# One product of 512 columns over high and low halves of the tokens in the gate of the second feed-forward network

## The chip, the cores and the metric

The kernel runs on one core of a Trainium2 chip. The metric is the device time of one execution in microseconds (us), the median of several runs. All matrix products are done on TensorE (PE); ScalarE (ACT) evaluates functions and copies, VectorE (DVE) does the element-wise arithmetic, SyncE (SP) issues the transfers of the weights and GpSimd (POOL) those of one further weight matrix.

## The reference

Two layers (`DEPTH = 2`) of a transformer block over 256 tokens with 1024 features. In each layer two gated feed-forward networks stand around a token mixing. Everything is float32. The part that the change touches is the gate `g` of the second network:

```python
def swiglu(h, w_gate, w_up, w_down):
    g = jnp.einsum('bsd,df->bsf', h, w_gate)
    u = jnp.einsum('bsd,df->bsf', h, w_up)
    return jnp.einsum('bsf,fd->bsd', jax.nn.silu(g) * u, w_down)

for l in range(DEPTH):
    h = modulate(rms_norm(x, norm_ffn1[l]), sh1, sc1)
    x = x + 0.5 * g1 * swiglu(h, w_gate1[l], w_up1[l], w_down1[l])
    h = modulate(rms_norm(x, norm_mix[l]), sh2, sc2)
    x = x + g2 * token_mixing(h, ...)
    h = modulate(rms_norm(x, norm_ffn2[l]), sh3, sc3)
    x = x + 0.5 * g3 * swiglu(h, w_gate2[l], w_up2[l], w_down2[l])
```

`D_FF` is 2816. The shifts, scales and gates (`sh1` to `g3`) are a product of `silu(c)` with `w_ada`, a matrix of 1024 x 9216 for each layer.

## The kernel before

**High and low parts.** A float32 product is made of three products in a reduced format (fp32r): each operand is split into a high part (rounded by ACT: `whi`, `hhi`, `guhi`) and a low part (the rest, by DVE: `wlo`, `hlo`, `gulo`), and `three` (L1282) adds high x high, high x low and low x high into one bank of PSUM. The stationary operand is the weight for the gate and the up product, the moving one is `hhi` or `hlo`, 128 features by 256 tokens, so each of these products has 256 columns.

**Steps.** Each feed-forward network is cut into 11 steps (`NF`) of 256 of its 2816 columns. `which` is 0 for the first network and 1 for the second. In a step i of the network (numbered from 0) PE does, in this order, the gate (48 products of 256 columns into bank `GB`), the up product (48 of 256 columns into `UB0` and `UB1`) and the down product (24 of 512 columns into four banks). Their weights come in three slots: slot 0 the gate's, slot 1 the up's, slot 2 the down's. Step 0 has another order of its own (`as_they_come`, banks `GB` and `SB_`), the last step puts two products between up and down (`spread_gate`), and steps 1 to 9 are a loop.

**ACT and DVE in a step.** Both engines do their work in the order in which it is written. In a step i > 0 of the second network ACT waits for the gate's end (`g_done`), evaluates silu over 512 columns of `GB` (L516), then rounds the down weights of this step (`split_hi(2)`, L464, a copy of 128 x 2048), then waits for DVE's product and rounds its first half to `guhi` (L520), rounds the gate weights of the next step (slot 0), and does the same for the second half and for slot 1. DVE weighs a chunk of `w_ada` first (`weigh_ada`, L801 and L803, 8 operations), then waits for `split_hi(2)` and makes the first half of `wlo[2]` (L997), waits for silu and for the first half of the up product, multiplies (L1002), waits for `guhi` and makes `gulo` (L1004), makes the second half of `wlo[2]` (L1006), then the same for the second half, and at last the low parts of slots 0 and 1 for the next step (L873). PE waits for the first `gulo` (`gulo_ready`, L1462) ahead of the down product, and for the low weights of slot 0 and 1 (`split_done`) ahead of gate and up.

**Late chunks.** In steps 0 and 1 of the second network DVE weighs a further chunk of `w_ada` (`weigh_late`, L850) between the low parts of slot 0 and slot 1. In layer 0 every step i > 0 begins with `weigh_ada`; in layer 1 steps 1 and 2 alone do.

Of the kernel before, what the change touches and what calls it, by code (L numbers as in the profile page):

```python
# [8 lines left out]
F32R = mybir.dt.float32r  # L9
BF16 = mybir.dt.bfloat16  # L10
I32 = mybir.dt.int32
ALU = mybir.AluOpType
ACT = mybir.ActivationFunctionType
AX_X = mybir.AxisListType.X

P = 128
# [19 lines left out]
def build(nc, x, c, w_ada, b_ada, norm_ffn1, w_gate1, w_up1, w_down1, norm_mix, w_in, qn_a, kn_a, qn_c, kn_c,  # L36
          g_out, w_out, norm_ffn2, w_gate2, w_up2, w_down2, out):
    _, S, D = x.shape
    L = w_in.shape[0]
    FF = w_gate1.shape[2]  # L40
    KT = D // P
    TT = S // P
    NF = FF // CW
# [42 lines left out]
    with ctx:  # L86
        def sb(name, shape, dt=F32):
            return ctx.enter_context(nc.sbuf_tensor(name, shape, dt))

        def sem(name):  # L90
            return ctx.enter_context(nc.semaphore(name))
# [6 lines left out]
        xs = sb("xs", [P, TT, D])  # L98
        xn = sb("xn", [P, TT, D])
        hTf = sb("hTf", [P, KT, S])  # L100
        hhi = sb("hhi", [P, KT, S], F32R)
        hlo = sb("hlo", [P, KT, S], F32R)
        gate = sb("gate", [P, D])
        room = sb("room", [P, 24, S])
        sqr = sb("sqr", [P, 2, S])
# [16 lines left out]
        eb = sb("eb", [P, GRP * (S + P)])  # L122
# [40 lines left out]
        mid_early = xn[:, 0, 0:2 * CW].rearrange("p (a n) -> p a n", a=2)  # L163
        silu = eb[:, 0:2 * S]
        guf = eb[:, 2 * S:4 * S]
        zf = hTf[:, :, :].rearrange("p k s -> p (k s)")
        z0 = zf[:, 0:GRP * S].rearrange("p (h s) -> p h s", h=GRP)
        z1 = zf[:, GRP * S:GRP * (S + P)].rearrange("p (h s) -> p h s", h=GRP)
# [9 lines left out]
        GB, UB0, UB1, SB_ = PS[4], PS[5], PS[6], PS[7]  # L178
# [55 lines left out]
        out_done = sem("out_done")  # L234

        g_done = sem("g_done")
        silu_ready = sem("silu_ready")
        u_done = sem("u_done")
        gu_ready = sem("gu_ready")
# [69 lines left out]
        def turn(l, n):  # L309

            return l * U_LAYER + n
# [141 lines left out]
        def _(act):  # L453
# [54 lines left out]
            def ffn_step(l, which, i, ahead, after, gated=False):  # L508
                base = turn(l, U_FFN[which])
                n = i + nth(l, 2 * NF, which * NF)  # L510
                act.wait_ge(g_done, n + 1)
                if gated:
                    act.activation(silu[:, 0:S], GB[:, 0:S], ACT.Silu)
                    act.activation(silu[:, S:2 * S], SB_[:, 0:S], ACT.Silu).then_inc(silu_ready, 1)
                else:
                    act.activation(silu, GB[:, :], ACT.Silu).then_inc(silu_ready, 1)  # L516
                split_hi(2, i + base)
                for ft in range(2):
                    act.wait_ge(gu_ready, n * 2 + ft + 1)
                    act.activation(guhi[:, ft * S:(ft + 1) * S], guf[:, ft * S:(ft + 1) * S], ACT.Copy).then_inc(guhi_ready, 1)  # L520
                    if after is not None:
                        split_hi(ft, i + after if ahead else after)
# [154 lines left out]
            for l in range(L):  # L677
# [49 lines left out]
                for n in range(NSLOT, len(OUT_CHUNKS)):  # L727
# [3 lines left out]
                    k = n % NSLOT  # L731
# [11 lines left out]
        def _(dve):  # L743
# [243 lines left out]
            def ffn_step(l, which, i, ahead, after, weighs=True, first=False, late=None):  # L987
                base = turn(l, U_FFN[which])
                n = i + nth(l, 2 * NF, which * NF)
                if which == 0 and not first:  # L990
                    weigh_ada([i + ada_turn(l, k, 0) for k in range(2)], [0, 1],
                              held[:, at_cols(i * (2 * CW) - 2 * CW, 2 * CW)].rearrange("p (a n) -> p a n", a=2))
                elif which == 1 and weighs and not first:
                    weigh_ada([i + ada_turn(l, 0, WF1 + 2)], [0], held[:, at_cols(i * CW + CW, CW)].rearrange("p (a n) -> p a n", a=1))

                dve.wait_ge(hi_full[2], i + (base + 1))
                dve.tensor_tensor(wlo[2][:, 0:D], raw[2][:, 0:D], whi[2][:, 0:D].bitcast(F32), ALU.subtract)  # L997
                dve.wait_ge(silu_ready, n + 1)
                for ft in range(2):
                    cut = slice(ft * S, (ft + 1) * S)  # L1000
                    dve.wait_ge(u_done, n * 2 + ft + 1)
                    dve.tensor_tensor(guf[:, cut], silu[:, cut], (UB0, UB1)[ft][:, 0:S], ALU.mult).then_inc(gu_ready, 1)  # L1002
                    dve.wait_ge(guhi_ready, n * 2 + ft + 1)
                    dve.tensor_tensor(gulo[:, cut], guf[:, cut], guhi[:, cut].bitcast(F32), ALU.subtract).then_inc(gulo_ready, 1)  # L1004
                    if ft == 0:
                        dve.tensor_tensor(wlo[2][:, D:2 * D], raw[2][:, D:2 * D], whi[2][:, D:2 * D].bitcast(F32), ALU.subtract).then_inc(split_done[2], 1)  # L1006
                if ahead:
                    split_lo(0, i + after)
                    if late is not None:
                        weigh_late(l, late)  # L1010
                    split_lo(1, i + after)
# [162 lines left out]
            for l in range(L):  # L1174
# [81 lines left out]
                for n in range(NSLOT, len(OUT_CHUNKS)):  # L1256
# [3 lines left out]
                    k = n % NSLOT  # L1260
# [11 lines left out]
        def _(pe):  # L1272
            pe.wait_ge(tables, 1)
            pe.wait_ge(rows_in, 5 * 16)
            for l in range(L):
                for k in range(KT):

                    o = (l * KT + k) * 13
                    last = pe.transpose(PS[0][:, o:o + 13], rows[:, l, k * P:(k + 1) * P], ident[0:13, 0:13])
            last.then_inc(cols_done, 1)  # L1280

            def three(ps, l_hi, l_lo, r_hi, r_lo, first, last):  # L1282

                pe.matmul(ps, l_hi, r_hi, start=first, stop=False)  # L1284
                pe.matmul(ps, l_hi, r_lo, start=False, stop=False)  # L1285
                return pe.matmul(ps, l_lo, r_hi, start=False, stop=last)  # L1286
# [137 lines left out]
            def ffn_step(l, which, i, is_last, first=False):  # L1424
                use = i + turn(l, U_FFN[which])
                n = i + nth(l, 2 * NF, which * NF)
                if first and (l > 0 or which > 0):
                    as_they_come(l, 2 * which, use, (GB, SB_)).then_inc(g_done, 1)
                elif not first:
                    pe.wait_ge(split_done[0], use + 2)  # L1430
                    wh, wl = chunk_cols(whi[0]), chunk_cols(wlo[0])
                    for ft in range(2):
                        for k in range(KT):
                            last = three(GB[:, ft * S:(ft + 1) * S], wh[:, k, ft * P:(ft + 1) * P], wl[:, k, ft * P:(ft + 1) * P],
                                         hhi[:, k, :], hlo[:, k, :], k == 0, k == KT - 1)
                    last.then_inc(g_done, 1)
                if first:
                    low_weights_last(use, UB0[:, 0:S]).then_inc(u_done, 1)
                else:
                    pe.wait_ge(split_done[1], use + 2)  # L1440
                wh, wl = chunk_cols(whi[1]), chunk_cols(wlo[1])
                for ft in range(1 if first else 0, 2):
                    for k in range(KT):
                        last = three((UB0, UB1)[ft][:, 0:S], wh[:, k, ft * P:(ft + 1) * P], wl[:, k, ft * P:(ft + 1) * P],
                                     hhi[:, k, :], hlo[:, k, :], k == 0, k == KT - 1)
                    last.then_inc(u_done, 1)
                if is_last:

                    pe.wait_ge(silu_ready, n + 1)
                    spread_gate(l, 2 * which, 0)  # L1450

                def down(ft, t, close):
                    tok = slice(ft * S + t * P, ft * S + (t + 1) * P)
                    for half in range(2):
                        w = slice(ft * D + half * HALF, ft * D + (half + 1) * HALF)
                        last = three(DB[2 * t + half][:, :], guhi[:, tok], gulo[:, tok], whi[2][:, w], wlo[2][:, w], first and ft == 0, close)
                        if close:
                            last.then_inc(d_done, 1)
                    return last


                pe.wait_ge(gulo_ready, n * 2 + 1)  # L1462
                if is_last:

                    spread_gate(l, 2 * which, 1)
                    down(0, 0, False)
                else:
                    for t in range(TT):
                        down(0, t, False)
                pe.wait_ge(split_done[2], use + 2)  # L1470
                pe.wait_ge(gulo_ready, n * 2 + 2)
                if is_last:
                    down(1, 0, True)
                    down(0, 1, False)
                    down(1, 1, True)
                else:
                    for t in range(TT):
                        down(1, t, False)
# [183 lines left out]
            for p in range(4):  # L1662
                last = gate_pair(p)
            last.then_inc(g_done, 1)
            pe.sem_inc(modc_done, 1)
            for l in range(L):
# [6 lines left out]
                for n in range(NC):  # L1673
# [5 lines left out]
                    if n == 3:  # L1679
# [3 lines left out]
                        for t in range(TT):  # L1683
                            last = pe.transpose(PVB[:, 8 + t * H_I:8 + (t + 1) * H_I], wiT[:, t * P:(t + 1) * P], ident[HD:KW, HD:KW])
# [39 lines left out]
                for n, (k0, nk) in enumerate(OUT_CHUNKS[:-1]):  # L1724
                    slot = n % NSLOT
                    pe.wait_ge(split_done[slot], turn(l, U_OUT + n // NSLOT) + 2)
                    if n == 0:

                        for low in (False, True):
                            for t in range(TT):  # L1730
                                pe.wait_ge(y_lo if low else y_hi, nth(l, 4, t + 1))
                                tok = slice(t * P, (t + 1) * P)
                                for half in range(2):
                                    w = slice(half * HALF, (half + 1) * HALF)
                                    if low:
                                        last = pe.matmul(DB[2 * t + half][:, :], hlo[:, k0, tok], whi[slot][:, w], start=False, stop=False)  # L1736
# [7 lines left out]
                    if n < 4:  # L1744
                        for t in range(TT):
                            last = out_block(n, t)
                        last.then_inc(out_done, 1)
                pe.wait_ge(y_lo, nth(l, 4, 4))
                for t in range(TT):
                    last = out_block(4, t)  # L1750
# [33 lines left out]
```

## Time and profile before

| | |
|---|---|
| Median of 3 runs | 1160.73 us (1159.63 to 1160.75) |
| Profiled execution | 1162.37 us |
| its span, first to last instruction | 1160.6 us |
| PE busy | 1132.1 us, 98% |
| DVE busy | 867.7 us, 75% |
| ACT busy | 530.2 us, 46% |
| TensorE clock, mean of the span | 0.992 of full |
| Products of 256 columns of `three` with the weight stationary | 3 x 1600 |

The busy shares are sums over the span; what an engine is worth in a stage is read from the timeline of the stage. The second network of layer 0 lies at about 404 to 593 us, that of layer 1 at about 966 to 1155 us. A duration of a matrix product in the timeline includes its way through the array; products overlap, so the rate is read from the distance of two starts.

### The profile page before, as it was taken

What the parts mean: (1) busy time and instruction counts of PE and PEld (TensorE: products, weight loads), DVE (VectorE), ACT (ScalarE), POOL (GpSimd) and SP (SyncE); (2) the same over time, 40 slices, a digit from 0 to 9 for tenths busy, and PEclk for the clock granted to TensorE, in tenths of its full rate; (3) what the DMA queues carried; (4) which work ended last, traced back from release to release, by engine and by line L of the source; (5) the groups of instructions that cost most, each with busy time, mean ns of one, the idle gap of its engine ahead of it and who ended that gap; (6) DMA issues with size and microseconds to landing.
All of it is one profiled execution on the core that took longest, in us unless ns stands there. A gap on an engine that the chain in (4) does not pass through costs nothing.

```text
span 1160.6 us, 20192 instructions
## 1 busy us (share of the span) xinstructions
PE 1132.1 (98%) x7890; PEld 1022.0 (88%) x7890; DVE 867.7 (75%) x1281; ACT 530.2 (46%) x685; POOL 64.5 (6%) x79
## 2 busy tenths in 40 slices
PE   6999999999999999999999999999999999999998
PEld 3699999989988799999989999997998878899997
DVE  5688788788986787766777787777888777845545
ACT  3433433555655653343364334435456555433432
POOL 2000110100000000000000101100000000000000
PEclk9999999999999999999989999998999999999999
DMA  9889889946532577777837898893943253756451
GB/s 304 282 287 319 293 296 331 314 128 214 182 99 91 174 234 252 251 236 257 270 129 256 294 333 297 296 348 114 299 146 128 92 181 113 235 196 211 154 196 73
DMA packets 160373, 258.43 MB, mean 223 GB/s; under 512 B 8365, under 2 KB 127277, under 8 KB 160319
## 3 DMA queue, kind: packets, MB, share of 16 engines
q1 hardware_dynamic: 140739, 182.25, 47.4%
q0 software_dynamic: 19584, 75.50, 19.4%
q8 instruction: 32, 0.52, 0.2%
q14 instruction: 18, 0.15, 0.0%
HBM read 256.56 MB, written 1.05 MB: 222 GB/s over the span
## 4 chain that ended last, share of the span: by engine, by line
PE 75%; DVE 12%; DMA 4%; ACT 3%; DVEq 3%; issue 2%; SPq 0%; ACTq 0%; POOLq 0%; POOL 0%
PE bank L1284 21%; PE bank L1286 20%; PE bank L1285 20%; DVE wlo L873 4%; DVE room L803 3%; DMA ada<-in_w_ada_dram 2%; PE bank L1628 2%; DVEq L805 1%; DMA raw<-in_w_gate_dram 1%; ACT whi L464 1%; PE bank L1547 1%; PE bank L1339 1%; PE bank L1375 1%; DMA xs<-in_x_dram 1%; PE bank L1404 1%
## 5 line engine op out<-in xcount | busy, mean ns | idle before, releaser
L1284 PE MATMUL bank<-hhi,whi 128*128 128x256 f32 (+1 forms) x1600 | 454.9, 284 | 0.0
L1286 PE MATMUL bank<-hhi,wlo 128*128 128x256 f32 (+1 forms) x1600 | 452.4, 283 | 0.0
L1285 PE MATMUL bank<-hlo,whi 128*128 128x256 f32 (+1 forms) x1600 | 452.2, 283 | 0.0
L464 ACT ACTIVATE whi<-raw 128x2048 fp32r<-128x2048 f32 (+1 forms) x174 | 321.7, 1851 | 9.8 <-PE bank L1736 5.3
L1284 PEld LDWEIGHTS bank<-hhi,whi 128*128 128x128 f32 (+1 forms) x1600 | 305.8, 191 | 4.0 <-issue 1.8
L1285 PEld LDWEIGHTS bank<-hlo,whi 128*128 128x128 f32 (+1 forms) x1600 | 305.9, 191 | 2.4 <-issue 0.5
L1286 PEld LDWEIGHTS bank<-hhi,wlo 128*128 128x128 f32 (+1 forms) x1600 | 305.8, 191 | 0.0
L873 DVE TENSOR_TENSOR wlo<-raw,whi 128x2048 fp32r<-128x2048 f32 (+2 forms) x130 | 281.9, 2197 | 12.1 <-ACT whi L464 10.7
L516 ACT ACTIVATE eb<-bank 128x512 f32<-128x512 f32 x40 | 23.9, 598 | 336.9 <-PE bank L1286 336.9
L803 DVE SCALAR_TENSOR_TENSOR room<-ada,cT,room 128x512 f32 (+3 forms) x252 | 159.5, 633 | 19.1
L997 DVE TENSOR_TENSOR wlo<-raw,whi 128x1024 fp32r<-128x1024 f32 x44 | 53.9, 1225 | 129.2 <-ACT whi L464 128.1
L1284 PE MATMUL bank<-whi,guhi 128*128 128x512 f32 x352 | 141.5, 402 | 1.7 <-DVE gulo L1004 1.7
L1285 PE MATMUL bank<-wlo,guhi 128*128 128x512 f32 x352 | 139.2, 395 | 0.0
L1286 PE MATMUL bank<-whi,gulo 128*128 128x512 f32 x352 | 139.2, 395 | 0.0
L422 POOL DMA_DIRECT2D ada<-in_w_ada_dram x64 | 56.3, 883 | 909.9 <-DVEq L837 758.9
L1284 PEld LDWEIGHTS bank<-whi,guhi 128*128 128x128 f32 x352 | 66.3, 188 | 17.8 <-DVE gulo L1004 2.5
L1286 PEld LDWEIGHTS bank<-whi,gulo 128*128 128x128 f32 x352 | 66.2, 188 | 16.1
L1285 PEld LDWEIGHTS bank<-wlo,guhi 128*128 128x128 f32 x352 | 66.2, 188 | 14.8 <-issue 1.0
L520 ACT ACTIVATE guhi<-eb 128x256 fp32r<-128x256 f32 x88 | 36.8, 418 | 87.3 <-DVE eb L1002 86.6
L1004 DVE TENSOR_TENSOR gulo<-eb,guhi 128x256 fp32r<-128x256 f32 x88 | 37.5, 426 | 42.6 <-ACT guhi L520 42.6
L1284 PE MATMUL bank<-whi,hhi 128*128 128x256 f32 (+1 forms) x184 | 60.5, 329 | 0.8 <-DVE wlo L873 0.8
L1285 PE MATMUL bank<-wlo,hhi 128*128 128x256 f32 (+1 forms) x184 | 58.0, 315 | 0.0
(224 smaller groups left out, 1164.5 us busy)
## 6 DMA issues: line engine op xcount, KB each, us to landing
ada<-in_w_ada_dram POOLq DMA_DIRECT2D x68, 1024.0 KB, 5.9
raw<-in_w_gate_dram SPq DMA_DIRECT2D x44, 1024.0 KB, 5.6
raw<-in_w_up_dram SPq DMA_DIRECT2D x44, 1024.0 KB, 7.0
raw<-in_w_down_dram SPq DMA_DIRECT2D x44, 1024.0 KB, 5.1
raw<-in_w_in_dram SPq DMA_DIRECT2D x28, 1024.0 KB, 6.4
raw<-in_w_out_dram SPq DMA_DIRECT2D x8, 512.0 KB, 3.3
raw<-in_w_out_dram SPq DMA_DIRECT2D x4, 1024.0 KB, 7.0
room<-in_w_ada_dram POOLq DMA_DIRECT2D x3, 1024.0 KB, 14.1
```

Source lines behind the costliest of these rows:

```text
L422: pool.dma_start(ada[:, slot, :, :], v_ada[:, row, col]).then_inc(ada_full[slot], 16)
L464: last = act.activation(dst, src, ACT.Copy)
L516: act.activation(silu, GB[:, :], ACT.Silu).then_inc(silu_ready, 1)
L520: act.activation(guhi[:, ft * S:(ft + 1) * S], guf[:, ft * S:(ft + 1) * S], ACT.Copy).then_inc(guhi_ready, 1)
L803: last = dve.scalar_tensor_tensor(sums, chunks[:, :, k, :], cT[:, k:k + 1], sums, ALU.mult, ALU.add)
L873: last = dve.tensor_tensor(dst, src, hi.bitcast(F32), ALU.subtract)
L997: dve.tensor_tensor(wlo[2][:, 0:D], raw[2][:, 0:D], whi[2][:, 0:D].bitcast(F32), ALU.subtract)
L1004: dve.tensor_tensor(gulo[:, cut], guf[:, cut], guhi[:, cut].bitcast(F32), ALU.subtract).then_inc(gulo_ready, 1)
L1284: pe.matmul(ps, l_hi, r_hi, start=first, stop=False)
L1285: pe.matmul(ps, l_hi, r_lo, start=False, stop=False)
L1286: return pe.matmul(ps, l_lo, r_hi, start=False, stop=last)
L1628: last = pe.matmul(PV_BANK[n][:, h * HD:(h + 1) * HD], probs(b, h), vs[:, b, off + h * HD:off + (h + 1) * HD], start=(b == 0), stop=(b == t))
```

## The change

In the second network (`which == 1`), steps 1 to 10 of both layers, the gate is computed in another way; step 0, the up and down products and the whole first network stay. `hhi` and `hlo` become two halves of one tile, side by side for each group of 128 features, so that they can be read as 512 moving columns. For each high weight one product of 512 columns then gives high x high in the first 256 columns of a bank and high x low in the other 256; low weight x high tokens, 256 columns, is added to the first 256. The two groups of 128 gate columns go to two banks, `GB` and `SB_`. The gate is then the sum of the two halves of each bank: ACT copies the second halves to a tile `gsum` in SBUF, DVE adds the first halves to it, and ACT evaluates silu over `gsum`.

```diff
-        hhi = sb("hhi", [P, KT, S], F32R)
-        hlo = sb("hlo", [P, KT, S], F32R)
+        both_h = sb("both_h", [P, KT, 2, S], F32R)
+        hhi, hlo = both_h[:, :, 0, :], both_h[:, :, 1, :]
...
+        gsum = eb[:, 4 * S:6 * S]
...
# ACT, ffn_step
+                elif which == 1:
+                    for ft in range(2):
+                        act.activation(gsum[:, ft * S:(ft + 1) * S], (GB, SB_)[ft][:, S:2 * S], ACT.Copy).then_inc(glow_read, 1)
+                    act.wait_ge(gsum_ready, i + l * (NF - 1))
+                    act.activation(silu, gsum, ACT.Silu).then_inc(silu_ready, 1)
                 else:
                     act.activation(silu, GB[:, :], ACT.Silu).then_inc(silu_ready, 1)
                 split_hi(2, i + base)
...
# DVE, ffn_step, behind weigh_ada
+                if which == 1 and not first:
+                    for ft in range(2):
+                        g = gsum[:, ft * S:(ft + 1) * S]
+                        dve.wait_ge(glow_read, i * 2 + (l * 2 * (NF - 1) + ft - 1))
+                        last = dve.tensor_tensor(g, (GB, SB_)[ft][:, 0:S], g, ALU.add)
+                    last.then_inc(gsum_ready, 1)
                 dve.wait_ge(hi_full[2], i + (base + 1))
                 dve.tensor_tensor(wlo[2][:, 0:D], raw[2][:, 0:D], whi[2][:, 0:D].bitcast(F32), ALU.subtract)
...
# PE, ffn_step, the gate
+                        cut = slice(ft * P, (ft + 1) * P)
                         for k in range(KT):
+                            if which == 1:
+                                bank = (GB, SB_)[ft]
+                                pe.matmul(bank[:, :], wh[:, k, cut], both_h[:, k, :, :].rearrange("p a s -> p (a s)"), start=k == 0, stop=False)
+                                last = pe.matmul(bank[:, 0:S], wl[:, k, cut], hhi[:, k, :], start=False, stop=k == KT - 1)
+                                continue
                             last = three(GB[:, ft * S:(ft + 1) * S], wh[:, k, ft * P:(ft + 1) * P], wl[:, k, ft * P:(ft + 1) * P],
                                          hhi[:, k, :], hlo[:, k, :], k == 0, k == KT - 1)
```

On PE, at the head of the loop over the second network's steps, the gate before, for one group of features:

```order
L1483 ISA
L1284 MATMUL bank<-hhi,whi 128x256
L1285 MATMUL bank<-hlo,whi 128x256
L1286 MATMUL bank<-hhi,wlo 128x256
L1284 MATMUL bank<-hhi,whi 128x256
```

and now, where both halves are named `both_h`:

```order
L1503 ISA
L1451 MATMUL bank<-both_h,whi 128x512
L1452 MATMUL bank<-both_h,wlo 128x256
L1451 MATMUL bank<-both_h,whi 128x512
L1452 MATMUL bank<-both_h,wlo 128x256
```

Sixteen pairs stand where sixteen triples stood; the columns streamed are the same.

On ACT, at the head of the same loop, before (`eb` holds silu, its product and now `gsum`; `bank` is PSUM):

```order
L527 UNCONDITIONAL_BRANCH
L527 ISA
L516 ACTIVATE eb<-bank 128x512
L460 ISA
L464 ACTIVATE whi<-raw 128x2048
L519 ISA
L520 ACTIVATE guhi<-eb 128x256
```

and now:

```order
L535 UNCONDITIONAL_BRANCH
L535 ISA
L520 ACTIVATE eb<-bank 128x256 x2
L522 ACTIVATE eb<-eb 128x512
L463 ISA
L467 ACTIVATE whi<-raw 128x2048
L527 ISA
L528 ACTIVATE guhi<-eb 128x256
```

Two copies stand ahead of silu, and silu and all behind it, the rounding of the down weights (L467) first, come behind a wait for DVE.

On DVE, in the same loop of layer 0, before:

```order
L801 TENSOR_SCALAR room<-ada,cT 128x256
L803 SCALAR_TENSOR_TENSOR room<-ada,cT,room 128x256 x7
L996 REGISTER_ALU
L997 TENSOR_TENSOR wlo<-raw,whi 128x1024
L1001 ISA
L1002 TENSOR_TENSOR eb<-eb,bank 128x256
```

and now:

```order
L809 TENSOR_SCALAR room<-ada,cT 128x256
L811 SCALAR_TENSOR_TENSOR room<-ada,cT,room 128x256 x7
L1007 ISA
L1008 TENSOR_TENSOR eb<-bank,eb 128x256 x2
L1010 REGISTER_ALU
L1011 TENSOR_TENSOR wlo<-raw,whi 128x1024
```

The two additions stand behind the eight operations of `weigh_ada` and ahead of the first half of `wlo[2]`.

## Rows read from the trace of the kernel before

**Rows 1.** The page: busy times, and the chain that ended last.

```profile
PE 1132.1 (98%) x7890; PEld 1022.0 (88%) x7890; DVE 867.7 (75%) x1281; ACT 530.2 (46%) x685; POOL 64.5 (6%) x79
PE 75%; DVE 12%; DMA 4%; ACT 3%; DVEq 3%; issue 2%; SPq 0%; ACTq 0%; POOLq 0%; POOL 0%
```

**Rows 2.** Timeline of PE, step 6, layer 0: start, duration (us), engine, line, operation.

```profile
506.17 0.28 PE L1284 MATMUL bank<-hhi,whi 128*128 128x256 f32 x1
...
511.91 0.28 PE L1284 MATMUL bank<-hhi,whi 128*128 128x256 f32 x1
...
517.55 0.28 PE L1286 MATMUL bank<-hhi,wlo 128*128 128x256 f32 x1
517.66 0.40 PE L1284 MATMUL bank<-whi,guhi 128*128 128x512 f32 x1
...
523.27 0.28 PE L1284 MATMUL bank<-hhi,whi 128*128 128x256 f32 x1
```

**Rows 3.** Timeline of ACT, the same step; in brackets its idle time and releaser.

```profile
512.11 0.60 ACT L516 ACTIVATE eb<-bank 128x512 f32<-128x512 f32 x1 [8.48 <-PE bank L1286]
512.60 1.90 ACT L464 ACTIVATE whi<-raw 128x2048 fp32r<-128x2048 f32 x1
516.12 0.42 ACT L520 ACTIVATE guhi<-eb 128x256 fp32r<-128x256 f32 x1 [1.62 <-DVE eb L1002]
```

**Rows 4.** Timeline of DVE, the same step.

```profile
514.53 1.23 DVE L997 TENSOR_TENSOR wlo<-raw,whi 128x1024 fp32r<-128x1024 f32 x1 [3.67 <-ACT whi L464]
515.68 0.41 DVE L1002 TENSOR_TENSOR eb<-eb,bank 128x256 f32<-128x256 f32 x1
516.58 0.43 DVE L1004 TENSOR_TENSOR gulo<-eb,guhi 128x256 fp32r<-128x256 f32 x1 [0.48 <-ACT guhi L520]
516.92 1.22 DVE L1006 TENSOR_TENSOR wlo<-raw,whi 128x1024 fp32r<-128x1024 f32 x1
```

**Rows 5.** Timeline of ACT, step 0; last, a group by line (count, busy, mean ns).

```profile
408.10 0.39 ACT L513 ACTIVATE eb<-bank 128x256 f32<-128x256 f32 x1 [0.67 <-PE bank L1409]
408.38 0.38 ACT L514 ACTIVATE eb<-bank 128x256 f32<-128x256 f32 x1
...
L627 ACT ACTIVATE hhi<-hTf 128x512 fp32r<-128x512 f32 x8 | 4.7, 624 | 5.6 <-DVE hTf L913 5.6
```

**Rows 6.** Timelines of DVE and PEld (weight loads), steps 0 to 3, layer 0.

```profile
410.59 1.23 DVE L997 TENSOR_TENSOR wlo<-raw,whi 128x1024 fp32r<-128x1024 f32 x1 [1.54 <-ACT whi L464]
...
428.58 1.23 DVE L997 TENSOR_TENSOR wlo<-raw,whi 128x1024 fp32r<-128x1024 f32 x1
...
442.57 3.84 DVE L803 SCALAR_TENSOR_TENSOR room<-ada,cT,room 128x256 f32 x7
446.63 1.23 DVE L997 TENSOR_TENSOR wlo<-raw,whi 128x1024 fp32r<-128x1024 f32 x1 [0.22 <-issue]
...
449.15 0.19 PEld L1284 LDWEIGHTS bank<-whi,guhi 128*128 128x128 f32 x1 [0.89 <-DVE gulo L1004]
...
463.24 1.23 DVE L997 TENSOR_TENSOR wlo<-raw,whi 128x1024 fp32r<-128x1024 f32 x1 [3.18 <-ACT whi L464]
```

**Rows 7.** Timeline of ACT: silu of steps 1, 2, 3 and 10, layer 0.

```profile
425.20 0.60 ACT L516 ACTIVATE eb<-bank 128x512 f32<-128x512 f32 x1 [8.41 <-PE bank L1286]
...
442.75 0.60 ACT L516 ACTIVATE eb<-bank 128x512 f32<-128x512 f32 x1 [7.97 <-PE bank L1286]
...
460.81 0.60 ACT L516 ACTIVATE eb<-bank 128x512 f32<-128x512 f32 x1 [7.99 <-PE bank L1286]
...
580.51 0.60 ACT L516 ACTIVATE eb<-bank 128x512 f32<-128x512 f32 x1 [8.48 <-PE bank L1286]
```

**Rows 8.** Timelines, last step of layer 0: PE between up and down; DVE behind.

```profile
586.07 1.88 PE L1347 MATMUL bank<-room,ones 128*128 128x512 f32 x4
...
588.05 1.29 DVE L865 TENSOR_TENSOR gate<-bank,LG 128x512 f32<-128x512 f32 x2 [0.27 <-PE bank L1347]
```

**Rows 9.** Windows: length; busy PE, PEld, DVE, ACT, POOL; clock; DMA share, GB/s.

```profile
237.00:242.00 5.00, 5.00 (x26) 3.86 (x26) 2.56 (x10) 1.45 (x5) 0.00 (x0) 0.66 0.00 0
1155.46:1159.40 3.94, 0.00 (x0) 0.00 (x0) 1.94 (x3) 0.00 (x0) 0.00 (x0) 1.00 0.60 243
1159.40:1160.60 1.20, 0.00 (x0) 0.00 (x0) 0.00 (x0) 0.00 (x0) 0.00 (x0) 0.54 0.19 75
```

## Prediction made before the change was run

> **What bounds the kernel now.** The page comes first: PE is busy for 98% of the span and holds 75% of the chain that ended last [rows 1]. A busy PE says little by itself, so the timeline of an ordinary step of the second network comes next: step 6 of layer 0. Gate, up and down follow each other without a gap: the gate's first product starts at 506.17, the up's at 511.91, the down's at 517.66, the next gate's at 523.27 [rows 2]. The step is 17.10 us long and all of it is PE's. The distance of two starts is (517.66 - 511.91) / 48 = 0.1198 us for 256 columns, and for 512 columns (523.27 - 517.66) / 24 = 0.234 us (the down product is 24 of them) [rows 2]. So time is taken by columns, and two products of 256 columns cost only 0.006 us more than one of 512.
>
> The third view is what PE would wait for if it were late: the first `gulo` ahead of the down product. Its chain in this step: silu at 512.11, rounding of the down weights at 512.60 [rows 3], first half of `wlo[2]` at 514.53 (DVE had stood idle for 3.67 us for it), product at 515.68, `gulo` at 516.58 for 0.43 us [rows 4], so it is there at 517.01. PE starts loading the first weights of the down product as the last up product starts, at 517.55 [rows 2]. The slack is about 0.5 us.
>
> The fourth view is the same chain in a step in which it is late. In step 2, DVE is still weighing `w_ada` (from 442.57 for 3.84 us), `wlo[2]` starts at 446.63 and PE's weight load for the down product stands idle for 0.89 us until 449.15, 2.52 us behind the start of `wlo[2]` [rows 6]. The step before and this one are 17.55 and 18.06 us long by silu's starts [rows 7], 0.45 and 0.96 us over 17.10. From this I take a rule of cost: let x be the start of L997; the down product behaves as if it started at x + 2.62, or where the up product ends, if that is later. In step 2 the up product ends at 442.75 - 0.20 + 5.75 = 448.30, and 446.63 + 2.62 - 448.30 = 0.95, which is the row's 0.96.
>
> **Part 1, the gate's products.** Removed are 48 starts of 256 columns, 5.74 us [rows 2]; added are 16 of 512 and 16 of 256. The mixture does not occur. With 0.234 and 0.1198 it takes 5.66 us; if PE's 256-column products cost half a 512 (0.117) once fewer instructions are queued, 5.61; bounds for the gain are 0 and 0.2 us. I take 5.61, a gain of 0.13 us in each of 20 steps, 2.6 us in all. The Trainium skill (TensorE: Matmul & The Clock Gate, Back-to-back issue gap) gives a warm product N/2.4 ns plus a fixed 2.5 ns; the rows differ from it (0.234 us where it has 0.216), and by it the gain would be 16 x 2.5 ns = 0.04 us for each step.
>
> **Part 2, the way to silu in an ordinary step.** Let A be the time at which ACT sees the gate's end. Before, silu starts at A, the rounding at A + 0.49, L997 at A + 2.42 [rows 3, 4]. Now: the first copy takes 0.39 us, the second starts 0.28 behind it [rows 5]; a handoff takes 0.03 us (512.60 + 1.90 to 514.53 [rows 3, 4]); the first addition starts at A + 0.42, the second 0.34 later (516.58 to 516.92 is that distance [rows 4]), and takes 0.41 us like the 256-column product with a PSUM operand [rows 4]: done at A + 1.17. Silu starts at A + 1.20. From SBUF 512 columns take 0.62 us [rows 5], and as now the next operation starts 0.11 before the end: rounding at A + 1.71, L997 at A + 3.64. That is 1.22 us later. DVE would otherwise be idle in that time (the 3.67 us above), so no work of its own is pushed. But queued behind ACT's new wait is the rounding of the down weights, and behind that, on DVE, the whole chain to `gulo`. PE has 517.66 - (514.53 + 2.62) = 0.51 us of slack [rows 2, 4] and then waits 0.71 us. With the gain of part 1 the step is 0.58 us longer: 17.68 us. From x to the next x by parts: 2.62 (start of down) + 5.61 + 5.61 + 0.20 + 3.64 = 17.68. The second `gulo` follows x by 4.9 us, PE wants it 2.7 us behind the start of the down product, at x + 5.3, so it costs nothing more; the low parts for the next gate are done at x + 7.1, wanted at x + 8.2. Bounds for the delay: 0.85 (the two copies and additions overlap better) to 1.6 us (a handoff of 0.15 us each).
>
> **Part 3, steps 1 and 2 with late chunks.** There DVE is the one that is late: L997 starts as soon as the weighing is done. The additions now stand in front of it, ACT's wait for them ends later still, and the rounding of the down weights, until now long done, begins only then: from the end of the weighing 0.34 + 0.41 + 0.03 + 0.51 + 1.93 = 3.22 us to L997, where it was 0. In step 1 x moves from 428.58 to 431.80; in step 2 by another 3.22, as the weighing there ends at a fixed distance behind the x of step 1 (446.63 - 428.58 = 18.05, all DVE's [rows 6]). PE then waits 3.8 us in step 1 and 4.3 us in step 2. Step 3 starts from PE again: x to x was 463.24 - 446.63 = 16.61 [rows 6] and becomes 17.68, 1.07 more. Bounds: 3.0 to 3.5 us for each of the two.
>
> **Part 4, the last step.** Between up and down PE has products of `spread_gate` (4 records, 1.88 us [rows 8]), the first half ahead of its wait for `gulo`. They cover the 1.22 us of delay within 0.2 us, so it drops out of the sum. DVE's end of the chain moves the gate's addition (588.05 [rows 8]) by 1.2, of which 0.3 us reach the residual; at the end of layer 0 PE's own work covers that, at the end of layer 1 it counts.
>
> **Sum for a layer.** 3.22 + 3.22 + 1.07 + 7 x 0.58 (x of steps 4 to 10) = 11.57; less 1.22 for the last step = 10.35 us. Layer 1 has the same two late chunks and the same distances; that its later steps don't weigh changes nothing, as DVE is ahead there. Both: 20.7, and 0.3 at the end: 21.0 us. The sum is made against the span of 1160.6 us; the profiled execution's own time, 1162.37, is 1.77 above its span and 1.6 above the median. A step's length is the same in all runs, so the difference goes onto the median: 1160.73 + 21.0 = 1181.7, say **1182 us**.
>
> **Rivals.** (a) The clock falls in the pauses. At the kernel's end PE rests from 1155.46; the granted clock is 1.00 until 1159.40 and mostly at half (1.2 GHz) in the 1.2 us behind [rows 9]: the trace shows a fall some 4 us into a rest. The pause of step 2 is 4.3 us, that of step 1 3.8. Where it fell elsewhere it stayed low for (1 - 0.66) x 5 x 2 = 3.4 us [rows 9]; a fall in step 2 costs half of that, 1.7 us (in step 1 DVE's chain covers it). One layer: 1183.7; both: 1185.4. The Trainium skill (TensorE: Matmul & The Clock Gate, HAM oscillation) describes just this, pauses between groups of products after which each group starts at half clock; by it both layers pay, 1185.4. (b) The delay is hidden, since PE's slack is larger than I read: then only part 1 is left, 2.6 us, and the time is 1158.1, faster. It decides at a slack of 1.22 us; the 0.89 us that PE did wait in step 2 speaks against. (c) Only the ordinary steps pay, because DVE reaches its additions earlier in steps 1 and 2 than I count: 20.7 less 2 x (3.22 + 3.22 - 1.16) = 10.1, 1171. (d) The product of 512 columns is no faster and the handoffs are slow: 1.6 us of delay, no gain: 2 x (3.5 + 3.5 + 1.6 + 7 x 1.1 - 1.6) = 29, 1190. (e) The change does nothing, the gate being built as before: 1160.7; the order of instructions shows it is not so.
>
> **How the numbers follow.** Forecast 0.60, (a) 0.22, (b) 0.03, (c) 0.07, (d) 0.06, (e) 0.02. The low bounds (0.85 us of delay, 3.0 for the late steps) give 2 x (3.0 + 3.0 + 0.7 + 7 x 0.2 - 0.85) = 14.5, 1175; the high ones (1.6 us, 3.5) give 2 x (3.5 + 3.5 + 1.5 + 7 x 0.96 - 1.6) = 27, 1188, and (a) lies within. The range is 1175 to 1188. Differences under 0.2% (2.3 us) can't be told from none: faster 0.03, same 0.02, slower 0.95.
>
> **What would show it.** In the changed profile PE's weight load ahead of the down product should stand idle in 18 steps with DVE's `gulo` as releaser, about 0.6 to 0.7 us in 14 of them and about 4 us in steps 1 and 2 of each layer; silu's starts should be 17.68 us apart; the gate's 32 products should take 5.6 us; ACT should stand in a wait for DVE ahead of silu. Step lengths of 17.0 in the second network would refute parts 2 and 3, an idle of 0.9 us in step 2 part 3 alone, a granted clock at half behind step 2 would be (a).

## The result and the profile after

The changed kernel took 1184.37 us in the median of 4 runs (1181.62 to 1187.43), the kernel before 1160.18 us (4 runs): 24.2 us more, a ratio of 1.021 (95% interval 1.0194 to 1.0227). The forecast was 1182, between 1175 and 1188.

The page of the changed kernel, against [rows 1]. PE has 6.5 us more of busy time in a span that is 23.0 us longer, and ACT holds 7% of the chain that ended last, where it held 3%:

```profile
span 1183.6 us, 19663 instructions
PE 1138.6 (96%) x7570; PEld 1010.7 (85%) x7570; DVE 883.4 (75%) x1321; ACT 544.5 (46%) x725; POOL 64.7 (5%) x79
PE 71%; DVE 12%; ACT 7%; issue 4%; DVEq 2%; DMA 2%; SPq 0%; ACTq 0%
```

The waits (total us, times, longest): the row that answers the question what PE waits for, first of the kernel before, then of the changed kernel. Before, this wait came 4 times and made 2.5 us; now it comes in all 18 steps of the two loops:

```profile
PEld bank L1284 <- DVE gulo L1004: 2.5, 4, 0.9
...
PEld bank L1298 <- DVE gulo L1018: 21.9, 18, 4.2
```

**An ordinary step** (step 7 of layer 0), timelines of ACT, DVE, PE's weight loads (PEld) and PE, against [rows 2 to 4]:

```profile
538.06 0.66 ACT L520 ACTIVATE eb<-bank 128x256 f32<-128x256 f32 x2 [7.78 <-PE bank L1452]
539.27 0.63 ACT L522 ACTIVATE eb<-eb 128x512 f32<-128x512 f32 x1 [0.55 <-DVE eb L1008]
539.80 1.90 ACT L467 ACTIVATE whi<-raw 128x2048 fp32r<-128x2048 f32 x1
...
538.48 0.76 DVE L1008 TENSOR_TENSOR eb<-bank,eb 128x256 f32<-128x256 f32 x2 [0.96 <-ACT eb L520]
541.74 1.22 DVE L1011 TENSOR_TENSOR wlo<-raw,whi 128x1024 fp32r<-128x1024 f32 x1 [2.50 <-ACT whi L467]
543.78 0.43 DVE L1018 TENSOR_TENSOR gulo<-eb,guhi 128x256 fp32r<-128x256 f32 x1 [0.48 <-ACT guhi L528]
...
544.25 0.19 PEld L1298 LDWEIGHTS bank<-whi,guhi 128*128 128x128 f32 x1 [0.69 <-DVE gulo L1018]
...
549.96 0.39 PE L1451 MATMUL bank<-both_h,whi 128*128 128x512 f32 x1
...
555.61 0.28 PE L1298 MATMUL bank<-both_h,whi 128*128 128x256 f32 x1
```

From ACT's first copy (538.06) to silu are 1.21 us, to the rounding of the down weights 1.74, to the first half of `wlo[2]` 3.68; before, the last was 2.42. DVE stands idle for 2.50 us for ACT's rounding, and ACT for 0.55 us for DVE's additions ahead of it. The first weight load of the down product stands idle for 0.69 us. The gate is 555.61 - 549.96 = 5.65 us long, where it was 5.74.

**Steps 1 and 2** of layer 0, against [rows 6, 7]: rows of DVE and of PE's weight loads (PEld) in turn, and at the end ACT's copies at the gate's end of steps 1, 2, 3 and 10:

```profile
431.90 1.23 DVE L1011 TENSOR_TENSOR wlo<-raw,whi 128x1024 fp32r<-128x1024 f32 x1 [2.50 <-ACT whi L467]
...
434.41 0.29 PEld L1298 LDWEIGHTS bank<-whi,guhi 128*128 128x128 f32 x1 [3.84 <-DVE gulo L1018]
...
449.94 0.76 DVE L1008 TENSOR_TENSOR eb<-bank,eb 128x256 f32<-128x256 f32 x2 [0.22 <-issue]
453.20 1.23 DVE L1011 TENSOR_TENSOR wlo<-raw,whi 128x1024 fp32r<-128x1024 f32 x1 [2.50 <-ACT whi L467]
...
455.71 0.19 PEld L1298 LDWEIGHTS bank<-whi,guhi 128*128 128x128 f32 x1 [2.79 <-DVE gulo L1018]
...
425.07 0.66 ACT L520 ACTIVATE eb<-bank 128x256 f32<-128x256 f32 x2 [8.22 <-PE bank L1452]
447.41 0.66 ACT L520 ACTIVATE eb<-bank 128x256 f32<-128x256 f32 x2 [9.33 <-PE bank L1452]
467.26 0.66 ACT L520 ACTIVATE eb<-bank 128x256 f32<-128x256 f32 x2 [7.87 <-PE bank L1452]
...
591.21 0.66 ACT L520 ACTIVATE eb<-bank 128x256 f32<-128x256 f32 x2 [7.88 <-PE bank L1452]
```

From the additions (449.94) to `wlo[2]` (453.20) are 3.26 us, in which DVE itself works for 0.76. The steps are 22.34 and 19.85 us long, where they were 17.55 and 18.06. Steps 3 to 10 are (591.21 - 467.26) / 7 = 17.71 us long, where they were 17.10.

### The profile page after: what moved, and what is told of

The parts are those of the page before. It is cut to its first block, busy times and chain, and to the rows that moved or that the text cites. A ratio compares the mean times of both kernels' runs of the same rounds, so it can differ in the third digit from the quotient of the medians.

```text
span 1183.6 us, 19663 instructions
## 1 busy us (share of the span) xinstructions
PE 1138.6 (96%) x7570; PEld 1010.7 (85%) x7570; DVE 883.4 (75%) x1321; ACT 544.5 (46%) x725; POOL 64.7 (5%) x79
## 4 chain that ended last, share of the span: by engine, by line
PE 71%; DVE 12%; ACT 7%; issue 4%; DVEq 2%; DMA 2%; SPq 0%; ACTq 0%
PE bank L1298 17%; PE bank L1299 16%; PE bank L1300 16%; PE bank L1451 5%; ACT whi L467 4%; DVE wlo L881 3%; PE bank L1452 3%; DVE room L811 2%; PE bank L1648 2%; DVEq L813 1%; PE bank L1567 1%; DVE eb L1008 1%; PE bank L1353 1%; DMA xs<-in_x_dram 1%; DVE gulo L1018 1%
## 5 line engine op out<-in xcount | busy, mean ns | idle before, releaser
L1298 PE MATMUL bank<-both_h,whi 128*128 128x256 f32 (+1 forms) x1280 | 365.1, 285 | 0.0
L1299 PE MATMUL bank<-both_h,whi 128*128 128x256 f32 (+1 forms) x1280 | 362.6, 283 | 0.0
L1300 PE MATMUL bank<-both_h,wlo 128*128 128x256 f32 (+1 forms) x1280 | 362.6, 283 | 0.0
L467 ACT ACTIVATE whi<-raw 128x2048 fp32r<-128x2048 f32 (+1 forms) x174 | 321.7, 1850 | 8.0 <-PE bank L1756 5.3
L1298 PEld LDWEIGHTS bank<-both_h,whi 128*128 128x128 f32 (+1 forms) x1280 | 245.2, 192 | 4.0 <-issue 1.8
L1299 PEld LDWEIGHTS bank<-both_h,whi 128*128 128x128 f32 (+1 forms) x1280 | 245.2, 192 | 1.4 <-issue 0.5
L1300 PEld LDWEIGHTS bank<-both_h,wlo 128*128 128x128 f32 (+1 forms) x1280 | 245.3, 192 | 0.0
L1298 PE MATMUL bank<-whi,guhi 128*128 128x512 f32 x352 | 144.9, 412 | 18.3 <-DVE gulo L1018 18.3
L1451 PE MATMUL bank<-both_h,whi 128*128 128x512 f32 x320 | 113.1, 396 | 0.0
L524 ACT ACTIVATE eb<-bank 128x512 f32<-128x512 f32 x20 | 12.0, 598 | 169.3 <-PE bank L1300 169.3
L1452 PE MATMUL bank<-both_h,wlo 128*128 128x256 f32 x320 | 89.8, 280 | 0.0
L520 ACT ACTIVATE eb<-bank 128x256 f32<-128x256 f32 x40 | 13.2, 381 | 161.8 <-PE bank L1452 161.8
```

The source lines that it names most:

```text
L467: last = act.activation(dst, src, ACT.Copy)
L1451: pe.matmul(bank[:, :], wh[:, k, cut], both_h[:, k, :, :].rearrange("p a s -> p (a s)"), start=k == 0, stop=False)
L1452: last = pe.matmul(bank[:, 0:S], wl[:, k, cut], hhi[:, k, :], start=False, stop=k == KT - 1)
```

## The experiments

The theory: the loss isn't the work added but where ACT's wait for DVE stands. The rounding of the down weights is queued behind it, on that waits DVE's `wlo[2]`, and on that the `gulo` which PE wants first. PE has 0.5 us of slack there in an ordinary step; in steps 1 and 2 DVE is late already, and there is none. The rivals: the wide product or the shared tile costs; it is the load on DVE; it is the clock.

**The changed kernel again,** beside the three that follow.

> The changed kernel again, beside the others of this group. Theory (the wait of ScalarE for VectorE holds back the rounding of the down weights, and with it the first low product that TensorE wants): 1184 us, ordinary steps of the second network 17.70 us, 0.6 to 0.7 us of TensorE's idle time in each and about 4 us in steps 1 and 2. Rival (the half clock seen behind step 1 in both layers makes the loss): the time goes with the mean granted clock from run to run, and a run without a fall would be near 1180.

It took 1184.33 us (1183.53 to 1185.97, 4 runs); the kernel before, over 19 runs in the same group, 1159.45 us; ratio 1.0228 (1.0211 to 1.0245). Ordinary steps were (592.82 - 468.96) / 7 = 17.69 us. The clock is not what makes the loss, but it takes part. Windows of this run (length; PE, PEld, DVE, ACT, POOL; clock; DMA share, GB/s), the last two rows behind the pauses of step 2 in layer 0 and in layer 1:

```profile
433.40:440.00 6.60, 5.34 (x13) 4.19 (x14) 5.56 (x8) 4.44 (x4) 0.00 (x0) 0.50 0.52 179
...
457.00:461.00 4.00, 4.00 (x12) 3.13 (x11) 3.52 (x5) 2.48 (x3) 0.00 (x0) 0.57 0.58 213
...
1027.00:1031.00 4.00, 4.00 (x12) 3.12 (x11) 3.52 (x4) 3.08 (x3) 0.00 (x0) 0.57 0.48 161
```

From the gate's end of step 1 to that of step 3 this run needs 43.65 us in layer 0 (425.31 to 468.96), the first profiled run of the changed kernel 42.19. The first profiled run had the clock down in step 1 alone (in layer 0 from 434 to 438 us, mean 0.57), this one in step 2 too. So a fall in step 1 was covered and one in step 2 cost 1.5 us, as rival (a) had it.

**The sum without the wide product.**

```diff
 # the kernel before, which == 1, steps 1 to 10; on PE the two groups of gate columns go to two banks
+    for ft in range(2):
+        act.activation(gsum[:, ft * S:(ft + 1) * S], (GB, SB_)[ft][:, 0:S], ACT.Copy).then_inc(glow_read, 1)
+    act.wait_ge(gsum_ready, i + l * (NF - 1))
+    act.activation(silu, gsum, ACT.Silu, scale=0.5).then_inc(silu_ready, 1)
 ...
+    last = dve.tensor_tensor(g, (GB, SB_)[ft][:, 0:S], g, ALU.add)
```

> The three products of 256 columns as before, but the way to silu as in the changed kernel: ScalarE copies the gate's 512 columns in two pieces, VectorE adds the bank to the copy, silu takes half of the sum. Theory: all of the loss is here, and the gain of the wide product is missing in the 16 steps in which TensorE's length counts, 16 x 0.09 = 1.5 us: 1186 us, ordinary steps 17.8 us. Rival (the wide product or the shared tile is what costs): near 1160.

1186.65 us (1185.65 to 1189.04, 4 runs), ratio 1.0249 (1.023 to 1.0268). Steps 3 to 10 are 17.84 us long (470.25 to 595.15 for seven). So the loss is there without the wide product and without the shared tile: all of it is on the way to silu.

**The wide product without the sum.** This kernel leaves the second halves of the banks, high x low, out of the gate.

```diff
 # the changed kernel, which == 1, steps 1 to 10
-    two copies, wait for gsum_ready, silu of gsum; on VectorE the two additions
+    act.activation(silu[:, 0:S], GB[:, 0:S], ACT.Silu)
+    act.activation(silu[:, S:2 * S], SB_[:, 0:S], ACT.Silu).then_inc(silu_ready, 1)
```

> The wide products alone: the second halves of the banks are left out of the sum, silu reads the first halves straight from the two banks, no copy, no addition, no wait for VectorE. Theory: the gate takes 5.66 us instead of 5.75, so 20 x 0.09 = 1.8 us less than before: 1158.4 us, ordinary steps 17.01 us. Rival (the wide product costs): above 1161. Rival (a wide product saves much more than the rows show): below 1155.

1157.93 us (1155.04 to 1159.35, 10 runs), ratio 0.9984 (0.9968 to 1.0). The wide product doesn't cost; it saves more in a step than was expected (0.20 us instead of 0.09). PE's timeline in an ordinary step, first and last pair of the gate and the first up product:

```profile
504.76 0.39 PE L1443 MATMUL bank<-both_h,whi 128*128 128x512 f32 x1
504.99 0.28 PE L1444 MATMUL bank<-both_h,wlo 128*128 128x256 f32 x1
505.10 0.40 PE L1443 MATMUL bank<-both_h,whi 128*128 128x512 f32 x1
...
510.31 0.28 PE L1290 MATMUL bank<-both_h,whi 128*128 128x256 f32 x1
```

The gate is 510.31 - 504.76 = 5.55 us long, 0.347 for a pair, and a step 16.90 us (493.61 to 510.51 at silu), 0.20 less than before. In the changed kernel, where PE waits in each step, the same pairs take 5.65 us.

**The rounding ahead of the wait.**

```diff
 # ACT, the changed kernel, which == 1, steps 1 to 10
     two copies
+    split_hi(2, i + base)
     act.wait_ge(gsum_ready, i + l * (NF - 1))
     act.activation(silu, gsum, ACT.Silu).then_inc(silu_ready, 1)
-    split_hi(2, i + base)
```

> The changed kernel with one move: ScalarE rounds the down weights right behind its two copies, ahead of the wait for VectorE and of silu. Theory: the first half of the low down weights starts 2.5 us behind the gate's end as seen by ScalarE instead of 3.6, silu is ready ahead of its use, TensorE doesn't wait in ordinary steps (17.0 us); in steps 1 and 2 the additions alone remain, 0.75 us each: 1160.2 - 1.8 + 4 x 0.75 = 1161.4 us. Rival (the load of 40 additions on VectorE makes the loss, not the order on ScalarE): above 1175.

1158.97 us (1157.07 to 1161.45, 10 runs), ratio 0.9998 (0.9985 to 1.0011). With the same instructions in another order the whole loss is gone. ACT and DVE in an ordinary step of this kernel:

```profile
513.63 0.66 ACT L520 ACTIVATE eb<-bank 128x256 f32<-128x256 f32 x2 [8.21 <-PE bank L1454]
514.17 1.92 ACT L467 ACTIVATE whi<-raw 128x2048 fp32r<-128x2048 f32 x1
515.98 0.63 ACT L523 ACTIVATE eb<-eb 128x512 f32<-128x512 f32 x1
...
514.04 0.76 DVE L1010 TENSOR_TENSOR eb<-bank,eb 128x256 f32<-128x256 f32 x2 [1.40 <-ACT eb L520]
516.12 1.23 DVE L1013 TENSOR_TENSOR wlo<-raw,whi 128x1024 fp32r<-128x1024 f32 x1 [1.32 <-ACT whi L467]
```

`wlo[2]` starts 2.49 us behind the gate's end instead of 3.68, the additions run while ACT rounds, and silu runs while DVE makes `wlo[2]`. The steps are 16.90 us long. In steps 1 and 2 only the additions themselves are left: 18.21 and 18.81 us against 17.55 and 18.06, 0.66 and 0.75 more; in layer 1 it is 1.02 and 0.74 more. These 3.2 us take up the 16 x 0.20 us that steps 3 to 10 gain, so the time is that of the kernel before.

**Steps 1 and 2 as before.**

```diff
 # the changed kernel; steps 1 and 2 of the second network are taken out of the loops
-    if which == 1:
+    if which == 1 and i not in (1, 2):
         the wide product, the copies, the wait and the additions
```

> The changed kernel, but steps 1 and 2 of the second network of both layers (those behind late chunks of VectorE's weighing) as before the change. Theory: ordinary steps stay 17.7 us, steps 1 and 2 are 17.6 and 18.1 as before, no pause of 4 us and no fall of the clock there: before + 2 x (1.07 + 7 x 0.6 - 1.2) + 0.3 = 1159.5 + 8.4 = 1168 us, so that steps 1 and 2 held some 16 us of the 24.9. Rival (all steps pay alike): 2 of 10 steps take a fifth of the loss away, 1179 us.

1167.21 us (1165.33 to 1172.23, 5 runs), ratio 1.0083 (1.0054 to 1.0113), the kernel before at 1160.02 in this group. Of the 24.9 us of the changed kernel (1184.33 less 1159.45), 17 are gone with 4 of its 20 steps (1184.33 less 1167.21).

**A delay below the slack.**

```diff
 # ACT, the kernel before, which == 1, steps 1 to 10
     act.activation(silu, GB[:, :], ACT.Silu).then_inc(silu_ready, 1)
+    act.activation(eb[:, 4 * S:5 * S], causal[:, :], ACT.Copy)
     split_hi(2, i + base)
```

> The kernel before with one copy of 128x256 from SBUF to SBUF on ScalarE between silu and the rounding of the down weights, in steps 1 to 10 of the second network: 0.33 us of delay in the chain to the first low product. Theory: below the slack of 0.51 us, so TensorE doesn't wait: ordinary steps 17.10 us, 1159.5 us. Rival (the delay counts from its first ns): 2 x 8 x 0.33 = 5.3 us more.

1158.88 us (1157.89 to 1160.18, 10 runs), ratio 0.9993 (0.9981 to 1.0006). Steps are 17.10 us long: 0.31 us later on ACT (511.67 to 511.98), and PE doesn't notice.

**A delay above the slack,** and nothing for DVE.

```diff
     act.activation(silu, GB[:, :], ACT.Silu).then_inc(silu_ready, 1)
+    act.activation(eb[:, 4 * S:6 * S].rearrange("p (a s) -> p a s", a=2), aliC[:, 0:2, :], ACT.Copy)
+    act.activation(sqr[:, :, :], aliC[:, 2:4, :], ACT.Copy)
     split_hi(2, i + base)
```

> As the run with one copy, but with two copies of 128x512, 1.02 us of delay and no work for VectorE or TensorE. Theory: 1.02 - 0.51 = 0.51 us of waiting in each ordinary step, 17.61 us; steps 1 and 2 as before, since VectorE is late there anyway; 2 x (1.0 + 7 x 0.51 - 1.0) + 0.2 = 7.3 us more: 1166.8 us. Rival (it is VectorE's additions, not the order on ScalarE): 1159.5 us.

1167.41 us (1166.22 to 1168.91, 4 runs), ratio 1.0067 (1.0041 to 1.0093). ACT in an ordinary step, and PE's weight load:

```profile
512.90 0.60 ACT L516 ACTIVATE eb<-bank 128x512 f32<-128x512 f32 x1 [7.99 <-PE bank L1289]
513.39 0.62 ACT L518 ACTIVATE eb<-aliC 128x512 f32<-128x512 f32 x1
513.91 0.62 ACT L519 ACTIVATE sqr<-aliC 128x512 f32<-128x512 f32 x1
514.43 1.90 ACT L464 ACTIVATE whi<-raw 128x2048 fp32r<-128x2048 f32 x1
...
518.89 0.19 PEld L1287 LDWEIGHTS bank<-whi,guhi 128*128 128x128 f32 x1 [0.47 <-DVE gulo L1007]
```

The rounding comes 1.53 us behind silu's start instead of 0.49, and the steps are 17.64 us long, 0.54 more. So 1.04 us of delay cost 0.54, and the slack is 0.50 us.

**The shared tile alone.**

```diff
 # the kernel before
-        hhi = sb("hhi", [P, KT, S], F32R)
-        hlo = sb("hlo", [P, KT, S], F32R)
+        both_h = sb("both_h", [P, KT, 2, S], F32R)
+        hhi, hlo = both_h[:, :, 0, :], both_h[:, :, 1, :]
```

> The kernel before with the high and low halves of the tokens in one tile, side by side, and nothing else. Both theories: nothing, 1159.5 us; the durations of the operations on both halves as before.

1159.6 us (1156.87 to 1164.13, 10 runs), ratio 1.0003 (0.9984 to 1.0023): nothing, with steps of 17.10 us.

**Three versions that keep the gain.** The first rounds ahead of the wait and leaves steps 1 and 2 as before; the second uses the wide product, the sum and the rounding first in both networks; the third is the second with steps 1 and 2 of the second network as before.

```diff
 # second version: the condition which == 1 falls away on PE, ACT and DVE (the third counts its waits otherwise)
-    if which == 1:
-        bank = (GB, SB_)[ft]
+    bank = (GB, SB_)[ft]
 ...
-    act.wait_ge(gsum_ready, i + l * (NF - 1))
+    act.wait_ge(gsum_ready, i + (2 * l + which) * (NF - 1))
```

> The changed kernel with the rounding of the down weights ahead of the wait for VectorE, and steps 1 and 2 of the second network as before the change. Theory: all steps 3 to 10 at 16.90 us instead of 17.10, steps 1 and 2 at 17.6 and 18.1: 16 x 0.20 = 3.2 us less than before: 1159.7 - 3.2 = 1156.5 us. Rival (the gain of the wide product is lost again behind the loop): 1159.7 us.

1157.75 us (1156.36 to 1161.45, 12 runs), ratio 0.9982 (0.9969 to 0.9996): 2.4 us less than before, where 3.2 were expected. That is hardly clear of the noise.

> The wide product, the sum of two halves and the rounding ahead of the wait, in all steps 1 to 10 of both networks of both layers. Theory: the first network gains 20 x 0.20 us, as VectorE stands idle for 1.6 us ahead of the low down weights there and the additions need 0.75; the second is as in the run that rounded first (1159.0): 1155 us. Rival (the first network's two chunks of weighing make VectorE late, as in steps 1 and 2 of the second): 1159 us or more.

1153.85 us (1153.33 to 1156.65, 6 runs), ratio 0.995 (0.9931 to 0.997). The steps of the first network are 16.90 us long too, at ACT's first copies in layer 0:

```profile
84.80 0.66 ACT L520 ACTIVATE eb<-bank 128x256 f32<-128x256 f32 x2 [8.21 <-PE bank L1452]
101.70 0.66 ACT L520 ACTIVATE eb<-bank 128x256 f32<-128x256 f32 x2 [8.21 <-PE bank L1452]
```

> As the run with all gates wide, but with steps 1 and 2 of the second network as before the change. Theory: 36 steps gain 0.20 us each: 1159.7 - 7.2 = 1152.5 us. Rival (VectorE is late in the first network): 1156.5 us or more.

1150.52 us (1149.69 to 1153.03, 6 runs), ratio 0.992 (0.9901 to 0.9939), with the kernel before at 1160.14 us in these three. The third version is 9.6 us faster than the kernel before and 34 us faster than the change as it was made.

## Why the prediction was right

**The slack and the rule for the down product's start.** The slack was taken as 0.51 us and measured as 0.50 by the longer delay, and the shorter one, 0.31 us, cost nothing. The weight load of the down product starts 2.51 us behind the start of `wlo[2]` in the rows after (541.74 to 544.25), where step 2 of before gave 2.52.

**The way to silu.** Predicted 3.64 us from the gate's end to `wlo[2]`, measured 3.68. The ordinary step came out at 17.71 us against a predicted 17.68.

**Steps 1 and 2.** Predicted 3.22 us from the end of the weighing to `wlo[2]`, measured 3.26. The predicted split, 4 x 3.22 = 12.9 of 21.0 us in 4 of 20 steps, is borne out by the run without them: 17 of 24.9 us were in these steps. Of the 4 us more, 2.9 are what the repeated run needs above the first profiled run from the gate's end of step 1 to that of step 3 (43.65 - 42.19 = 1.46 us in layer 0, 43.92 - 42.47 = 1.45 in layer 1), with the clock down in step 2. The pauses came out at 3.84 us in step 1 (3.8 predicted) and at 2.79 in step 2 where 4.3 was forecast. The step before explains the second: with the clock down behind step 1's pause, PE itself was later at the end of step 2's up product, and waited that much less. The run with the sum alone shows it: in its layer 0 the clock stayed up in step 1 (1.00 from 435.7 to 440 us), and the pause of step 2 was 4.14 us; in its layer 1 the clock fell in step 1, and the pause was 2.49. The distance between the starts of `wlo[2]`, 453.20 - 431.90 = 21.30 us, is what was worked out, 18.05 + 3.22 = 21.27.

**The wide product.** Taken as 0.13 us for each step, from 5.61 us for the gate. In the changed kernel the gate is 5.65, so this term was 0.04 too large there. Without the pauses it is 0.20, my upper bound. By the rule of the Trainium skill (TensorE: Matmul & The Clock Gate, Back-to-back issue gap) the estimate was 0.04 us; neither kernel agrees with it (0.09 us in the changed one, 0.20 without the pauses).

**The sum.** From the gate's end of step 1 to that of step 10 it gave 10.35 us a layer, and 0.13 more without step 1's gain, 10.5. The first profiled run shows 166.14 - 155.31 = 10.8 in layer 0 and 11.2 in layer 1; in layer 1 DVE stood idle for 0.43 us within the weighing of step 1. The repeated run shows 12.2 and 12.8. Both had the same steps 3 to 10; what the second had more is the clock in step 2.

**The last step.** It was to cost nothing, and did: from the gate's end of step 10 in layer 0 to the first of the 32 products behind the last step PE needs 593.38 - 580.51 = 12.87 us before and 604.15 - 591.21 = 12.94 after. At the end of layer 1 0.3 us were forecast; from that gate's end to the end of the span it is 18.2 us in both.

**Chance in the total.** Between the gate's end of step 10 in layer 0 and that of step 1 in layer 1 the first profiled run takes 998.94 - 591.21 = 407.7 us, the repeated one 995.65 - 592.82 = 402.8, the kernel before 987.21 - 580.51 = 406.7. The first had the clock down there for some 14 us (608 to 612, 806 to 814, 840 to 844), the repeated one for some 3 (808 to 812), the kernel before for some 14. So the repeated run lost 25.0 us in the two layers against that profile, and its span is longer by 21.3 us only. That one execution comes near the forecast says less than the steps do.

**What was mis-sized** is the chance of rival (a), the clock's fall in the pauses, at 0.22. In all three traces with the late pauses (the changed kernel twice, and the sum alone) it fell near a pause in both layers, and in two of the three, in both layers, behind step 2, where it is paid for with 1.5 us. Rival (a) for both layers was priced at 1185.4 and the forecast without it at 1181.7. The medians, 1184.37 and 1184.33, lie between them, nearer to the rival. The mean clock was 0.985 to 0.990 in the 8 runs of the changed kernel, 0.991 to 0.996 in the 19 of the kernel before in the first group, and within the 8 the time goes with it: 1181.62 us at 0.990, 1187.43 at 0.985. How much of that comes from the pauses isn't shown: the first profiled run, which paid for no fall in step 2, took 1185.3 us, the repeated one, which paid in both layers, 1183.53. A fall in step 1 is covered by DVE's chain, as said: the sum alone needs 43.64 us from the gate's end of step 1 to that of step 3 in layer 0, where the clock fell in step 2 only, and 43.78 in layer 1, where it fell in both. The Trainium skill (TensorE: Matmul & The Clock Gate, HAM oscillation) names such pauses as the place where the half clock is paid for, and the repeated run agrees with it (clock 0.57 in the windows of 4 us behind them). Not every pause does: in the sum alone PE's weight loads rested 3.64 us in step 1 of layer 0, and no fall followed.

**The other rivals.** (b), a delay that is hidden, falls with the two delays: below 0.5 us nothing is paid, above it what exceeds 0.5 us. (d), no gain and slow handoffs with a delay of 1.6 us, falls too: the delay was 3.68 - 2.42 = 1.26 us, and the wide product does gain. (c), nothing paid in steps 1 and 2, falls with the run in which these steps are as before.

**Left open.** Why the pairs take 5.55 us where PE never waits and 5.65 where it waits once in a step was not tried. Nor can the falls of the clock at other places (840 to 844 us in the first profiled run of the changed kernel, none there in the profile before) be put down to the change, and so the clock's part of the 24 us has no number of its own.

## What to carry to other kernels

A wait that is added to an engine delays everything queued behind it, so look down the queue for the first result that another engine is short of, and put that ahead of the wait: here one moved call was worth 25 us, and the added work itself cost 0.7 to 1.0 us in each of the four steps where it was not covered, and nothing elsewhere. A delay costs only what exceeds the slack, and where an engine is already late there is no slack, so price such steps apart. Read the slack from an ordinary step and the price of a wait from a step in which the trace already has one.

## What the runs showed of the hardware

A product of 512 columns with one of 256 takes 0.347 us where PE never waits (5.55 / 16, the products alone), three of 256 columns take 0.359 (5.74 / 16, the kernel before), both with the clock at its upper level. The gain of a wider product is small here, 3% of the gate, and is lost as soon as PE has to wait for the halves to be added.

The clock's fall isn't tied to a length of the rest that can be read off. In the changed kernel's repeated run it fell within the rest of 3.85 us in step 1: the rest began at 434.66 - 3.85 = 430.81, and the clock is at half from 433.40 on, 2.6 us into it, where the prediction had read a fall some 4 us into the rest at the kernel's end. In step 2 of that run it fell only when PE had already resumed behind a rest of 1.95 us; in the first profiled run, layer 0, not at all behind one of 2.79, and in the sum alone not behind one of 3.64. In the two rows from the repeated run, PE's weight loads that end the rests:

```profile
434.66 0.29 PEld L1298 LDWEIGHTS bank<-whi,guhi 128*128 128x128 f32 x1 [3.85 <-DVE gulo L1018]
...
455.97 0.19 PEld L1298 LDWEIGHTS bank<-whi,guhi 128*128 128x128 f32 x1 [1.95 <-DVE gulo L1018]
```

In the kernel that rounds first, whose rests in these steps are 1.25 to 1.72 us, no fall came near them.
